# Forget-gate page attention: decay matmuls of both head pairs ahead of the scores, decay loads from ScalarE's queue

## The reference, cut to what matters

```
c = jnp.cumsum(logf.astype(F32), axis=1)
s = jnp.einsum('bqgrd,blgd->bqgrl', qg, kf) + (c_q - c_k[:, None])
p, _ = masked_softmax(s, (kpos[None, :] <= pos[:, None])[None, :, None, None, :])
return (jnp.einsum('bqgrl,blgd->bqgrd', p, vf).reshape(B, Q, H, D),)
```

## Time and profile before

| | us |
|---|---|
| Median of 3 runs | 3758.71 (3750.97 to 3761.93) |
| The profiled execution | 3766.02 |
| Its span, first to last instruction | 3764.5 |
| TensorE busy in the span | 3208.9 (85%) |
| VectorE busy | 1454.6 (39%) |
| ScalarE busy | 1003.8 (27%) |
| GpSimd busy | 593.1 (16%) |
| Mean granted TensorE clock | 0.904 of full speed |

### The profile page before, as it was taken

How to read it: one execution, slowest core, us unless ns; L and a number is a source line. 1 busy time by engine, 2 the same in 40 slices (tenths; PEclk the granted TensorE clock), 3 DMA queues, 4 the chain that set the end, 5 groups by cost and what they waited for, 6 DMA issues and landing times. The chain is left out here.

```text
span 3764.5 us, 67506 instructions
## 1 busy us (share of the span) xinstructions
PE 3208.9 (85%) x22697; PEld 2126.9 (56%) x22697; DVE 1454.6 (39%) x4231; ACT 1003.8 (27%) x2410; POOL 593.1 (16%) x946
## 2 busy tenths in 40 slices
PE   8999997999999898996655758899878867889869
PEld 4454447888888555563424533466555544556533
DVE  3100112444443355553224547321146653555423
ACT  1000001223322456662102321100035542333311
POOL 0000002222220000002014635000001112333200
PEclk9979998999999589996668988999979987999989
DMA  5533646444441222144437955422252218999642
GB/s 191 180 118 123 218 150 155 123 125 125 119 126 38 72 67 80 49 101 122 159 114 250 304 189 201 157 94 91 56 154 63 63 36 276 326 320 305 243 152 84
DMA packets 333801, 556.88 MB, mean 148 GB/s; under 512 B 73170, under 2 KB 215802, under 8 KB 329786
## 3 DMA queue, kind: packets, MB, share of 16 engines
q1 hardware_dynamic: 256132, 347.69, 29.4%
q0 software_dynamic: 54000, 173.90, 14.6%
q10 hardware_dynamic: 23340, 30.98, 2.4%
HBM read 490.66 MB, written 118.25 MB: 162 GB/s over the span
## 5 line engine op out<-in xcount | busy, mean ns | idle before, releaser
L330 PE MATMUL PS<-even_w,even_xT 128*128 128x512 f32 (+1 forms) x1152 | 499.3, 593 | 1.6 <-DMA even_w<-in_w_in_e 1.6
L1132 PE MATMUL PS<-cmp_xT,cmp_w 128*128 128x255 f32 (+2 forms) x2176 | 487.4, 375 | 1.1 <-DVEq L1211 1.1
L1132 PEld LDWEIGHTS PS<-cmp_xT,cmp_w 128*128 128x128 f32 x2176 | 393.9, 191 | 47.6 <-issue 1.2
L1022 ACT ACTIVATE cmp_xT<-PS 64x512 f32<-64x512 f32 x260 | 155.0, 596 | 941.2 <-PE PS L1103 939.7
L330 PEld LDWEIGHTS PS<-even_w,even_xT 128*128 128x128 f32 x1152 | 223.7, 197 | 259.2 <-issue 253.2
L1022 DVE COPY cmp_xT<-PS 64x512 f32<-64x512 f32 x260 | 179.2, 689 | 295.5 <-PE PS L1103 293.6
L330 PE MATMUL PS<-odd_w,odd_xT 128*128 128x368 f32 x896 | 286.5, 475 | 1.4 <-DVE odd_xT L279 1.4
L286 DVE COPY even_o<-PS 128x512 f32<-128x512 f32 (+3 forms) x81 | 50.3, 621 | 449.7 <-PE PS L330 433.4
L330 PEld LDWEIGHTS PS<-odd_w,odd_xT 128*128 128x128 f32 x896 | 167.9, 191 | 99.4 <-issue 3.2
L1040 POOL DMA_DIRECT2D cmp_pairs<-in_cache_nsa x256 | 151.6, 599 | 393.0 <-issue 379.1
L1764 POOL DMA_DIRECT2D s_fox_kv<-in_cache_fox x256 | 137.6, 538 | 313.1 <-issue 287.8
(11 more groups left out here) (443 smaller groups left out, 4736.3 us busy)
## 6 DMA issues: line engine op xcount, KB each, us to landing
s_fox_kv<-in_cache_fox POOLq DMA_DIRECT2D x256, 256.0 KB, 7.3
s_fox_kv<-in_cache_fox SPq DMA_DIRECT2D x256, 256.0 KB, 7.5
cmp_pairs<-in_cache_nsa POOLq DMA_DIRECT2D x256, 128.0 KB, 3.0
cmp_pairs<-in_cache_nsa SPq DMA_DIRECT2D x256, 128.0 KB, 2.8
s_sel_kv<-in_cache_nsa POOLq DMA_DIRECT2D x256, 128.0 KB, 4.9
s_sel_kv<-in_cache_nsa SPq DMA_DIRECT2D x256, 128.0 KB, 5.0
out_dil_sample<-in_cache_dil_w SPq DMA_DIRECT2D x8, 4088.0 KB, 23.6
even_w<-in_w_in_e SPq DMA_DIRECT2D x8, 2048.0 KB, 8.2
```

The lines of the kernel that those rows point to most:

```text
L330: last = nc.tensor.matmul(bank(c, t, 128)[:, 0:n], xT[:, k, t * 128:t * 128 + 128], w[:, c % WS, k, 0:n], start=(k == 0), stop=(k == KT - 1))
L1022: last = nc.vector.tensor_copy(dst, x) if l else nc.scalar.activation(dst, x, ACT.Copy)
L1132: last = nc.tensor.matmul(hidden_ps(x, NK)[:, g], w1[:, kv, c, :], xT[:, u % 2, kv, g, c % 8, at:at + NK], start=(c == 0), stop=(c == 15))
```

## The change

The decays of both pairs are computed first, in one group of eight matmuls that begins the accumulation; the scores then add to it. The decays are held twice, once for each pair, the second copy one row quarter further on: pair p, quarter j reads partitions from 32((j+p) mod 4). That takes eight DMAs for a batch row instead of four. All decay loads move from SP's queue to ScalarE's: those of batch rows 0 and 1 to the start of ScalarE's part of the first block, the others to the second iteration of each batch row, between the exponentials and the copy of the probabilities. The decay group waits for the exponentials of both pairs of the round before, and stands ahead of the wait for the key copies.

```diff
-            dec = sb("dec", [128, 2, RB, KW])
+            dec = sb("dec", [128, 2, P, RB, KW])
...
+        def decay_rows(p, j):
+
+            return 32 * ((j + p) % 4)
+
         def load_decay(eng, b):
             if b >= 2:
                 eng.wait_ge(scored, RB * P * (b - 1))
             v = E.decay[b].rearrange("h (k j n) -> j h k n", k=RB, j=4)
-            for j in range(4):
-                eng.dma_start(dec[32 * j:32 * j + 16, b % 2], v[j]).then_inc(dec_in[b % 2], 16)
+            for p in range(P):
+                for j in range(4):
+                    at = decay_rows(p, j)
+                    eng.dma_start(dec[at:at + 16, b % 2, p], v[j]).then_inc(dec_in[b % 2], 16)
...
-                        load_decay(sp, 0)
-                        load_decay(sp, 1)
...
                 @block.scalar
                 def _(act):
+                    if fox:
+                        load_decay(act, 0)
+                        load_decay(act, 1)
                     act.wait_ge(sn_ok, 1)
...
                 for r in range(US // 4, NR, 2):
-                    if fox and r % RB == US // 4 and 2 <= r // RB + 1 < DEC_BATCH:
-                        load_decay(sp, r // RB + 1)
                     load(sp, r)
...
                 def scores(r):
                     b = r // RB
+                    if fox:
+                        if r % RB == 0:
+                            hold(dec_in[b % 2], 64 * P * (b // 2 + 1))
+                        hold(expd, r * P)
+                        for j in range(4):
+                            for p in range(P):
+                                rows = slice(decay_rows(p, j), decay_rows(p, j) + 16)
+                                nc.tensor.matmul(PS[32 * j:32 * j + 32, s_bank(r * P + p)], hsel[rows, p, :], dec[rows, b % 2, p, r % RB, :], start=True, stop=False)
                     for e in range(2):
                         hold(tcopied[e], 2 * r + 2)
-                    if fox and r % RB == 0:
-                        hold(dec_in[b % 2], 64 * (b // 2 + 1))
                     for p in range(P):
                         x = r * P + p
-                        hold(expd if fox else s_free, x - 1)
+                        if not fox:
+                            hold(s_free, x - 1)
                         for j in range(4):
-                            last = nc.tensor.matmul(PS[32 * j:32 * j + 32, s_bank(x)], q[:, p, b, :], kT[:, p, j, :], start=True, stop=not fox)
-                        if fox:
-                            for j in range(4):
-                                rows = slice(32 * j, 32 * j + 16)
-                                last = nc.tensor.matmul(PS[32 * j:32 * j + 32, s_bank(x)], hsel[rows, p, :], dec[rows, b % 2, r % RB, :], start=False, stop=True)
+                            last = nc.tensor.matmul(PS[32 * j:32 * j + 32, s_bank(x)], q[:, p, b, :], kT[:, p, j, :], start=not fox, stop=True)
                         last.then_inc(scored, 1)
...
                     if it < NR:
                         probs(it)
+                    if fox and it % RB == 1 and 2 <= it // RB + 1 < DEC_BATCH:
+                        load_decay(act, it // RB + 1)
                     if 0 <= it - 1 < NR:
                         copy_probs(it - 1)
```

## The result

The changed kernel took 3782.86 us (median of 6 runs, 3771.4 to 3796.57) against 3755.68 us before (median of 6, 3750.97 to 3761.93): ratio 1.0072, 95% interval 1.0048 to 1.0095. It is slower, by less than 1%. On the 3758.7 us of the prediction that is +27 us (+18 to +36); forecast was +16, with a range up to 3806.

A forecast was written before the change was run, and what follows sets the result against it. TensorE's own work plus one hand-over from ScalarE was taken to set the round. Terms -36 (matmuls) +34 (issues) +11 (clock) +7 (start) gave +16 us, 3775 us on the median 3758.7; range 3752 to 3806.

The forecast's parts named there:

- The decay matmuls (-36): TensorE's rounds: all eight decay matmuls run at once, saving 0.56 us in each of 64 rounds, 36 us.
- Rival 2: Decay group on TensorE: the eight matmuls run four at a time, gaining only 9 us; +43, 3802 us; chance 0.17.
- Rival 5: Decay group: row quarters take turns at a bank, matmuls run one by one, 195 us more, 3970; chance 0.02.
- The issues (+34): ScalarE's queue ahead of the probabilities copy: eight decay-load issues take 5.6 us without cover, six times, 34 us.
- Rival 3: ScalarE's decay-load issues are cheap, a set 2.9 us, and the clock may hold; -12, 3747 us; chance 0.11.
- The clock (+11): TensorE behind each of six stalls: about half speed for some 4.5 us, costing 1.8 us each, 11 us.
- Rival 1: TensorE's clock holds behind the stalls and the stage's start costs nothing; -5, 3754 us; chance 0.14.
- The start (+7): Stage's start: doubled decay bytes delay TensorE's first rounds, partly offset by SP's earlier pages; +7 us, bounds -8 and +10.
- So the pages stay hidden: Page loads in the rounds: DMA's 53.3 us per eight rounds fits within TensorE's 57.5, so doubled decays cost nothing there.
- rival 4: Page loads in the rounds: pages come late as three queues share the engines; another 10 to 20 us, 3790; chance 0.06.

The follow-up runs named there:

- e3: The kernel before with only the new matmul order: decays of both pairs first, from one copy in shared row quarters, loads untouched on SP; ratio 0.9975.
- e8: The kernel before with its four decay loads a batch row issued by ScalarE at the changed kernel's places; ratio 1.0062.
- e6: The changed kernel with 44 unread transposes ahead of the values in the six stalled rounds, to keep TensorE busy; ratio 1.0080.
- e4: The kernel before with only the decay loads doubled, eight DMAs from SP, the second copy never read; ratio 1.0065.
- e7: e5 with batch row 1's decays loaded in the loop during batch row 0 instead of at the start; ratio 0.9938.
- e1: The changed kernel with all decay loads, still eight DMAs and two copies, back at their old places in SP's queue; ratio 1.0036.
- e2: The changed kernel with ScalarE's eight loop issues spread, two at the end of each of four iterations; ratio 1.0018.
- e5: e2 with each copy holding only the eight heads of its own pair, so decay matmuls have 8 rows; ratio 0.9960.
- e10: The changed order with one copy, heads of two j mixed per row quarter; ScalarE issues one DMA in each of four iterations, batch row 1's in the loop; ratio 1.0002.

## Why the prediction was right, and where its sum was off

**The decay matmuls (-36): right.** Eight ran as one group, and clean rounds fell by 0.53 us, the ones with merge work by up to 0.92; 38.3 us over 62 rounds, 0.62 each where 0.56 was forecast. Round 0 and the first transposes add 5.0, which no term had. (The 446 us that the prediction gives the stage are its rounds; the stage is 496.9.) Rival 2 (four at a time) is what e3 shows for shared quarters, 0.13 a round where the working had 0.14; it doesn't hold for the change. Rival 5 is out by the same rows: separate row quarters wrote one bank together. The rule of the Trainium skill weighed there (TensorEngine Tiling (Array Packing), Restrictions and Gotchas) does not hold for four row quarters in different partitions of one bank, on this chip.

**The issues (+34): right in place, 3 us high.** Eight issues took 6.0 us in the round shown, 0.4 above the 5.6 expected; but two ran beside the exponentials, so that a gap grew by 5.2 on average and six by 31.3. e8 shows the same mechanism alone, with half the issues. Rival 3 (cheap issues) is out: a set cost 6.0, and it needed under 3.0.

**The clock (+11): right.** 11.4 us behind the six stalls, by clean rounds; two of the six are taken like the other four. In e6, where TensorE works through the gap, the rounds behind five of them are clean. Rival 1 (the clock holds) is out. Not foreseen was the clock behind merges, 1.5 us more than before: the wait of 1.85 us for VectorE's scaling was followed by slow clock in two of seven merge rounds after and in one before (the earlier trace rows has the same waits).

**The start (+7): 8.7.** e4 has it without ScalarE, e8 has ScalarE without it, e7 takes it away by one set fewer. So it was the packets of the decays, as argued. SP's earlier begin gave back 2.0 us: with SP asking for them (e1) the start was 50.1.

**"So the pages stay hidden": the step that failed.** The prediction let the doubled decays cost nothing in the rounds as long as the average of a batch row had room (53.3 of 57.5 us). e4 says 20.4 us for the doubling alone. An average over 55 us hides that the decays land in a short time, at a far lower rate, and it knew nothing of the idle time without a name. In the changed kernel pages did stay hidden but for 1.4 us, so rival 4 did not come about there; but the idle time without a name went from 3.1 to 10.9 us, and with the clock lost behind it and small waits the others above clean grew from 6.3 to 17.8, +11.5. The prediction did say that without the stall the DMA would bind; e1 and e2 show page waits of 5.3 and 12.0 us, and more idle time without a name beside them.

So the forecast of +16 against +22.3 in the profiled stage misses, with its sign: matmuls -2 (and -5 in round 0 and the first transposes), issues -3, start +2, and for nothing priced the clock behind merges +1.5, the others above clean +11.5, tail +1. That is 10 us one way and 16 the other: the sum lies nearer to the result than its terms do, and that part is luck. The 27 us of the timed ratio lie 5 above the stage of one profile, inside the interval.

## What to carry to other kernels

When DMA issues move to a compute engine's queue, put them where that engine waits anyway: the same loads ahead of a copy that TensorE waits for cost 31 us plus 11 of clock, behind it no stall of TensorE (e2). A second copy of a small operand, made so that matmuls can run side by side, must be paid for in DMA: count the packets and look at the outermost dimension, not at the bytes alone (e5 halved the bytes and its decays took as long to land as e2's), and look at the microseconds in which they land rather than at the average. And a kernel that was stalled can hide the next bound: here undoing the stalls alone (e1) gave back 15.6 us of the 42.7 that the stalls had cost.

## What the runs showed of the hardware

- Eight decay matmuls, over all four row quarters and all four column quarters, each used twice, into two banks: 0.59 us to the next group's start, as much as four. With both decay matmuls of a j in the same square of the array (e3), 0.99 us.
- A DMA whose outermost dimension is 2 moved 48 GB/s and held SP's queue for 4 us a piece, where one of 16 rows took 0.65 us to issue.
- Packets of ScalarE's queue in flight at once: up to 23 for decay loads of 16 rows, up to 13 for those of 8 rows (e5), up to 4 where the outermost dimension was 2 (e10).
- TensorE idle times of up to 4.4 us that no semaphore explains, 79 of 0.5 us or more in the rounds of the fourteen traces, each ended 1.2 to 1.9 us behind a 16 KB packet on the queue named "instruction"; about 3 us in all before, 11 after, 24 in e1.
- A wait of 1.85 us was followed by a mean clock of about 0.6 over the next 4 us in one of seven merges before (round 60) and two of seven after (rounds 20 and 28), and by full clock at the same place in others, with the same wait (rounds 20 and 52 before). What decides it was not found.
